# Layer 0's prompt attention with its values product turned round: values stationary, both branches' factors spread by a matmul

## The reference

```
o = g[..., 0:1] * o_cmp + g[..., 1:2] * o_slc + g[..., 2:3] * o_win
```

## Time and profile before

| | us |
|---|---|
| median of 3 runs | 3194.72 |
| lowest, highest | 3194.48, 3202.56 |
| the profiled execution | 3194.32 |
| its span, first to last instruction | 3192.5 |
| PE busy | 3044.4 (95%) |
| DVE busy | 1032.4 (32%) |
| ACT busy | 604.7 (19%) |
| POOL busy | 631.1 (20%) |
| prompt attention, first scores to first `z_total` matmul | 608.15 to 885.02 |

### The profile page before, as it was taken

One profiled execution on the slowest core, in us unless ns is written; L12 is line 12 of the kernel. 1 busy time (PEld: TensorE's weight loads), 2 busy tenths in 40 slices (PEclk: granted clock), 3 DMA queues, 4 the chain that ended last, 5 costly groups with the idle time before them and its releaser, 6 DMA issues.

```text
span 3192.5 us, 43230 instructions
## 1 busy us (share of the span) xinstructions
PE 3044.4 (95%) x18443; PEld 2762.8 (87%) x18443; DVE 1032.4 (32%) x2161; ACT 604.7 (19%) x1016; POOL 631.1 (20%) x298
## 2 busy tenths in 40 slices
PE   7999999999987999999999998988999999999997
PEld 5866767788844999999999998977899999999997
DVE  2003135665533342222222224065342122222224
ACT  3002111454432220000000003044220000000003
POOL 1020000000010232232232222202322223223220
PEclk9999999999998999999999999988999999999998
DMA  5634410210041311111111111100011111111111
GB/s 161 191 84 123 139 50 1 78 47 1 1 142 56 107 40 40 53 41 40 42 52 40 40 53 34 43 17 14 18 50 40 40 53 40 40 53 40 40 50 60
DMA packets 209617, 180.15 MB, mean 56 GB/s; under 512 B 36746, under 2 KB 190399, under 8 KB 208834
## 3 DMA queue, kind: packets, MB, share of 16 engines
q1 hardware_dynamic: 202416, 149.32, 15.6%
q0 software_dynamic: 6848, 28.04, 3.0%
q10 hardware_dynamic: 162, 0.04, 0.0%
HBM read 162.97 MB, written 19.51 MB: 57 GB/s over the span
## 4 chain that ended last, share of the span: by engine, by line
PE 87%; DVE 6%; SPq 3%; issue 2%; ACT 2%; DMA 1%; DVEq 0%; ACTq 0%
PE ps L1962 52%; PE ps L586 7%; PE ps L711 4%; PE ps L1411 3%; PE ps L1978 3%; PE ps L582 3%; PE ps L1381 2%; PE ps L1394 2%; PE ps L2343 2%; SPq L979 1%; SPq L977 1%; DVE arena L2056 1%; PE ps L2327 1%; PE ps L2206 1%; DVE arena L2072 1%
## 5 line engine op out<-in xcount | busy, mean ns | idle before, releaser
L1962 PE MATMUL ps<-spot,w_hi 128*128 128x368 f32 (+1 forms) x6828 | 1324.0, 328 | 18.5 <-DVE spot L2174 15.8
L1962 PEld LDWEIGHTS ps<-spot,w_hi 128*128 128x128 f32 x6828 | 1156.4, 188 | 23.0 <-DVE spot L2174 19.4
L1962 PE MATMUL ps<-spot,w_lo 128*128 128x368 f32 (+1 forms) x3468 | 763.7, 328 | 0.0
L1962 PEld LDWEIGHTS ps<-spot,w_lo 128*128 128x128 f32 x3468 | 599.1, 188 | 0.0
L1939 POOL CAST w_hi<-arena 128x2048 fp32r<-128x2048 f32 x79 | 153.6, 1944 | 1424.4 <-DMA arena<-in_w_gate_up 776.5
L1940 POOL TENSOR_TENSOR w_lo<-arena,w_hi 128x2048 fp32r<-128x2048 f32 x79 | 367.9, 4657 | 6.3
L2072 DVE TENSOR_TENSOR arena<-arena,ps 128x368 f32<-128x368 f32 x336 | 158.7, 528 | 486.2 <-PE ps L1962 460.1
L586 PE MATMUL ps<-arena 128*128 128x368 f32 (+1 forms) x768 | 244.2, 476 | 1.5 <-DVE arena L1210 1.5
L586 PEld LDWEIGHTS ps<-arena 128*128 128x128 f32 x768 | 146.5, 193 | 87.7 <-issue 5.5
L2149 ACT ACTIVATE arena<-arena 128x1088 f32<-128x1088 f32 x44 | 49.0, 1114 | 894.5 <-DVEq L2165 894.5
L2169 DVE TENSOR_TENSOR arena<-arena,ps 128x368 f32<-128x368 f32 x132 | 62.4, 528 | 446.9 <-PE ps L1962 441.8
(11 more groups left out here) (429 smaller groups left out, 2719.6 us busy)
## 6 DMA issues: line engine op xcount, KB each, us to landing
arena<-in_w_gate_up SPq DMA_DIRECT2D x88, 512.0 KB, 4.5
arena<-in_w_down SPq DMA_DIRECT2D x22, 1024.0 KB, 4.9
arena<-in_cache_nsa_cmp_kv SPq DMA_DIRECT2D x128, 128.0 KB, 2.2
arena<-in_cache_nsa_slc_kv SPq DMA_DIRECT2D x128, 128.0 KB, 2.5
arena<-in_w_in_even SPq DMA_DIRECT2D x9, 1024.0 KB, 6.3
x_spill<-arena POOLq DMA_DIRECT2D x1, 4352.0 KB, 14.9
arena<-in_x_prompt SPq DMA_DIRECT2D x8, 512.0 KB, 7.0
arena<-in_cmp_w_k POOLq DMA_DIRECT2D x16, 256.0 KB, 4.4
```

The lines of the kernel that those rows point to most:

```text
L1962: mm = nc.tensor.matmul(ps[:, 3 * s + j, 0:b - a], w, x[:, a:b], start=m == 0, stop=m == len(order) - 1)
```

## The change

The values product has its operands swapped: the 64 values of a key head are stationary (`v_of`) and the turned probabilities are moving. The result has head columns on partitions, g = 0 in PSUM's lower and g = 1 in its upper half, and tokens along the free axis. The values of a whole unit, both g by turns for each key tile, stand in one segment: behind the turn of chunk 0 and ahead of that of chunk 1.

The column of ones is gone. ACT's exponential sums up the denominators itself (`accum_out`, into `den4`). DVE's `factor_rows` makes reciprocal times gate of them, and PE's `factors` spreads these to the turned layout with four matmuls, whose stationary operand is a factor column repeated 64 times and whose moving one is the identity. ACT copies them to SBUF (`fac`). DVE's `finish` multiplies both branches by them in one product. The compressed matmul stands by itself (`compressed`) and ACT copies its result to `oN` (`base`). POOL adds the two branches and then adds them to `oN`, and gives `at_oT`. `mix`, `out`, POOL's copies and memsets and the semaphore `v_ones` go. PE's loop ends two steps earlier. SP waits in addition for the first `at_oT` ahead of its `dec_late` load, and DVE for the last `at_o` ahead of its first write to `rstd` in the decode attention, since `fac` lies in that tile.

```diff
--- before.py
+++ after.py
@@ -1296,15 +1296,17 @@
         ob = [at(h0 + 2 * T + 5376 + k * 256, 2, P) for k in range(2)]
         knew = at(16768, 2, TS)
         negm, scal = small[:, 0:8], small[:, 16:24]
+        fac = [rstd[:].rearrange("p a b -> p (a b)")[:, 256 * k:256 * (k + 1)] for k in range(2)]
+        den4 = [small[:, 24 + 4 * k:28 + 4 * k] for k in range(4)]
         loads["bias_in"] = [(bias_s, const["bias_slc"]), (bias_w, const["bias_win"])]
         UNITS = [(r, i, br) for r in range(R0) for i in range(PT) for br in range(2)]
 
         VA = HD + 2
 
-        def v_ones(br, i, g):
-
-            c = 256 * br + g * VA
-            return kvt[:, i, c:c + HD + 1]
+        def v_of(br, i, g):
+
+            c = 256 * br + P + g * HD
+            return kvt[:, i, c:c + HD]
 
         def key_tiles(u):
 
@@ -1331,17 +1333,16 @@
 
         def attn_pool(pool, E):
             pool.wait_ge(stored, 16 * stores[0])
-            pool.wait_ge(sem("kt_tr"), 2)
-            for br in range(2):
-                c = 256 * br
-                for g in range(G):
-                    E.chain(nc.gpsimd.tensor_copy(kvt[:, 0:PT, c + g * VA:c + g * VA + HD],
-                                                  kvt[:, 0:PT, c + P + g * HD:c + P + (g + 1) * HD]))
-                for g in range(G):
-                    nc.gpsimd.memset(kvt[:, 0:PT, c + g * VA + HD:c + g * VA + HD + 1], 1.0).then_inc(sem("v_ones"), 1)
             pool.wait_ge(sem("kt_s"), 1)
             for b in range(2):
                 window_load(pool, b)
+            for ri in range(len(UNITS) // 2):
+                r, i, _ = UNITS[2 * ri]
+                o = oN[:, r, toks(i)]
+                pool.wait_ge(sem("at_o"), ri + 1)
+                E.chain(nc.gpsimd.tensor_tensor(ob[ri % 2][:, 0], ob[ri % 2][:, 0], ob[ri % 2][:, 1], ALU.add))
+                pool.wait_ge(sem("at_base"), ri + 1)
+                nc.gpsimd.tensor_tensor(o, o, ob[ri % 2][:, 0], ALU.add).then_inc(sem("at_oT"), 1)
 
         def window_load(e, b):
             src = d["state_nsa_win_kv"][0, b].rearrange("(j p) a g e -> p j a (g e)", p=P)
@@ -1395,43 +1396,56 @@
                                                  sp3[u % 3][:, g, b * P:(b + 1) * P], ident[:])
                     mm.then_inc(sem(f"at_tr{g}"), 1)
 
-            def values(u, g):
+            def compressed(ri):
+                r, i, _ = UNITS[2 * ri]
+                if ri == 0:
+                    step_wait(pe, "dve", "pc")
+                if ri >= 2:
+                    pe.wait_ge(sem("at_o"), ri - 1)
+                nc.tensor.matmul(ps[:, 6 + ri % 2, 256:384], vbd[:, r], pcT[:, i], start=True, stop=True)\
+                    .then_inc(sem("at_cmp"), 1)
+
+            def values(u):
                 r, i, br = UNITS[u]
                 ri = u // 2
-                pe.wait_ge(sem(f"at_copied{g}"), first_chunk[u + 1])
-                if br == 0 and g == 0:
-                    if ri == 0:
-                        pe.wait_ge(sem("v_ones"), 4)
-                        step_wait(pe, "dve", "pc")
-                    if ri >= 2:
-                        pe.wait_ge(sem("at_oT"), ri - 1)
+                for g in range(G):
+                    pe.wait_ge(sem(f"at_copied{g}"), first_chunk[u + 1])
+                if br == 0:
+                    pe.wait_ge(sem("at_base"), ri + 1)
                 j0, n = key_tiles(u)
-                c = (2 * br + g) * VA
                 for j in range(n):
-                    mm = nc.tensor.matmul(ps[:, 6 + ri % 2, c:c + HD + 1], pt2[u % 2][:, g, j], v_ones(br, j0 + j, g),
-                                          start=j == 0, stop=j == n - 1)
+                    for g in range(G):
+                        mm = nc.tensor.matmul(ps[g * HD:(g + 1) * HD, 6 + ri % 2, br * P:(br + 1) * P], v_of(br, j0 + j, g),
+                                              pt2[u % 2][:, g, j], start=j == 0, stop=j == n - 1)
                 mm.then_inc(sem("at_pv"), 1)
 
-            def mix(ri):
-                r, i, _ = UNITS[2 * ri]
-                pe.wait_ge(sem("at_o"), ri + 1)
-                out = ps[:, 6 + ri % 2, 384:512]
-                nc.tensor.matmul(out, vbd[:, r], pcT[:, i], start=True, stop=False)
+            def factors(ri):
+
+                pe.wait_ge(sem("at_s"), ri + 1)
                 for br in range(2):
-                    mm = nc.tensor.matmul(out, ob[ri % 2][:, br], ident[:], start=False, stop=br == 1)
+                    for g in range(G):
+                        k = 4 * (ri % 2) + 2 * br + g
+                        mm = nc.tensor.matmul(ps[g * HD:(g + 1) * HD, 6 + ri % 2, (2 + br) * P:(3 + br) * P],
+                                              scal[:, k:k + 1].to_broadcast([P, HD]), ident[:], start=True, stop=True)
                 mm.then_inc(sem("at_ot"), 1)
 
-            for step in range(n_units + 5):
+            for step in range(n_units + 3):
                 if step < n_units:
                     score(step)
-                if step >= 6 and step % 2 == 0:
-                    mix(step // 2 - 3)
                 n_turn = len(chunks(step - 2)) if 2 <= step < n_units + 2 else 0
-                for c in range(2):
-                    if c < n_turn:
-                        turn(step - 2, c)
-                    if 3 <= step < n_units + 3:
-                        values(step - 3, c)
+                base = step // 2 - 1 if step % 2 == 0 and 2 <= step < n_units + 2 else None
+                if n_turn:
+                    turn(step - 2, 0)
+                if base is not None and n_turn < 2:
+                    compressed(base)
+                if step >= 3:
+                    values(step - 3)
+                    if step % 2 == 0:
+                        factors(step // 2 - 2)
+                if n_turn == 2:
+                    turn(step - 2, 1)
+                    if base is not None:
+                        compressed(base)
             pe.wait_ge(sem("z_summed"), R0 - 1)
             for k, (a, b) in enumerate(SPLIT):
                 mm = nc.tensor.matmul(ps[:, 2 + k, 0:b - a], ones[:], z_sum[:, a:b], start=True, stop=True)
@@ -1443,7 +1457,7 @@
             j, n = chunks(u)[c]
             e.wait_ge(sem(f"at_tr{g}"), k + 1)
             if u >= 2 and c == 0:
-                e.wait_ge(sem("at_pv"), 2 * (u - 2) + g + 1)
+                e.wait_ge(sem("at_pv"), u - 1)
             copy(pt2[u % 2][:, g, j:n], ps[:, 4 + g, 0:(n - j) * P].rearrange("p (j t) -> p j t", j=n - j))\
                 .then_inc(sem(f"at_copied{g}"), 1)
 
@@ -1472,20 +1486,26 @@
                 v.tensor_tensor_reduce(sp3[u % 3][:, g, 0:n], scores(u, g), bias[:, g, bias.shape[2] - n:], -1.0, -NEG,
                                        ALU.add, ALU.min, negm[:, m:m + 1]).then_inc(sem("at_scored"), 1)
 
-            def finish(ri):
+            def factor_rows(ri):
 
                 r, i, _ = UNITS[2 * ri]
-                dve.wait_ge(sem("at_pv"), 4 * ri + 4)
-                got = ps[:, 6 + ri % 2, 0:4 * VA].rearrange("p (k e) -> p k e", k=4)
+                dve.wait_ge(sem("at_exp"), 4 * ri + 4)
                 s = scal[:, 4 * (ri % 2):4 * (ri % 2) + 4]
-                ch(v.reciprocal(s, got[:, :, HD]))
+                if ri >= 2:
+                    dve.wait_ge(sem("at_ot"), ri - 1)
+                ch(v.reciprocal(s, den4[ri % 4]))
                 s4 = s.rearrange("p (b g) -> p b g", b=2)
                 gt = gates[:, i].rearrange("p (g r k) -> p k g r", g=G, r=R0)[:, 1:3, :, r]
-                ch(v.tensor_tensor(s4, s4, gt, ALU.mult))
+                v.tensor_tensor(s4, s4, gt, ALU.mult).then_inc(sem("at_s"), 1)
+
+            def finish(ri):
+
+                dve.wait_ge(sem("at_pv"), 2 * ri + 2)
+                dve.wait_ge(sem("at_fac"), ri + 1)
                 if ri >= 2:
-                    dve.wait_ge(sem("at_ot"), ri - 1)
-                v.tensor_tensor(ob[ri % 2].rearrange("p b (g e) -> p (b g) e", g=G), got[:, :, 0:HD],
-                                s.unsqueeze(2).to_broadcast([P, 4, HD]), ALU.mult).then_inc(sem("at_o"), 1)
+                    dve.wait_ge(sem("at_oT"), ri - 1)
+                v.tensor_tensor(ob[ri % 2].rearrange("p b t -> p (b t)"), ps[:, 6 + ri % 2, 0:2 * P], fac[ri % 2], ALU.mult)\
+                    .then_inc(sem("at_o"), 1)
 
             def new_rows():
                 dve.wait_ge(sem("kt_w"), 1)
@@ -1510,6 +1530,8 @@
                         score(step, c)
                     if 2 <= step < n_units + 2 and c < len(chunks(step - 2)):
                         copy_chunk(dve, v.tensor_copy, step - 2, c, 0)
+                if step >= 3 and step % 2 == 1 and step < n_units + 2:
+                    factor_rows(step // 2 - 1)
                 if step >= 5 and step % 2 == 1:
                     finish(step // 2 - 2)
                 if step in Z_STEPS:
@@ -1533,22 +1555,33 @@
                 n = key_tiles(u)[1] * P
                 act.wait_ge(sem("at_scored"), 2 * u + g + 1)
                 m = 2 * (u % 4) + g
```

(28 more changed lines are left out.)

## The result

| | before | after |
|---|---|---|
| median, us | 3197.22 (4 runs) | 3159.77 (4 runs, 3153.26 to 3165.99) |
| profiled execution, us | 3194.32 | 3159.47 |
| its span | 3192.5 | 3157.6 |
| first scores to first `z_total` matmul | 608.2 to 885.0: 276.8 | 613.0 to 853.0: 240.0 |

The ratio is 0.9889, 95% interval 0.9869 to 0.9910: 1.1% faster. The forecast was 3158 us. The median of before grew by one run measured beside the new ones; the forecast's 36.6 us was made against the profiled execution, and the profiled executions differ by 34.9.

What follows compares the result with a forecast made beforehand. PE's instruction stream was taken to bound the prompt attention. Values -56.5, passages +15.4, mix against factors -3.5 and new waits +8 made -36.6 us from the profiled 3194.32: forecast 3158 us, range 3144 to 3180.

Steps and rivals of the forecast that it cites:

- The values: Prompt attention's values with operands swapped: 1056 records at 0.0545 us in place of 0.108, saving 56.5 us.
- Rival (b): Halves don't overlap in the values: a record costs its 0.109 us stream, 3221 us, or load and stream, 3292; chance 0.05.
- the prediction's test of a round: PE's pieces in an attention round before, scores, transposes, values and mix, summed to 67.4 us; the third round took 68.5.
- The passages: PE's changes of matmul form around the values segment: 96 more at 0.16 us, +15.4 us; bounds 5 and 32.
- rival (c): Each passage costs PE the weight loader's 0.33 us: +16 us, 3174 us; chance 0.10.
- Factors against mix: PE drops 128 records that turned `ob`, 14.4 us, and adds 256 factor records at 0.0545 us, 14.0 us.
- Waits: PE's 3.1 us wait for `finish` goes; new waits for DVE in the attention add 8 us, bounds 2 and 18.
- rival (a): DVE takes PE's place as bound: score loops 0.5 us dearer in 32 large steps, +16 us, 3174 us; chance 0.10.
- part 7: New PE waits for DVE in large score steps, round-start bias scalings and gate products: 8 us together.
- ACT and POOL: Attention's sum readings at 0.186 us and copies on ACT, 64 sums of 0.3 to 0.7 us on POOL: all hidden.
- Behind the attention: Decode stage after `z_total`, led by SP's 80 page loads, moves as a whole, length unchanged; gain passed on in full.
- Rival (d): Decode stage gives the gain back if its loads, not `z_total`, set its end: about 3190 us; chance 0.05.

Runs made afterwards that it cites:

- block order: Changed kernel with all key tiles of g = 0 first, then all of g = 1, in the values: attention 269.1 us, median 3182.25 us.
- single half: Block-order kernel with both g of the values sent to the lower half of the array's columns, upper half's values left out: attention 290.8 us.

## Why the prediction was right

**The values (-56.5).** A record has the pitch read from the decode attention, 0.055 us. This is a property of form and order together, as the block order (+29 us) and the single half (+51 us) show. The change alternates, like the line in the earlier trace rows from which the prediction took its number, so the number was right; how much of it hung on the order the prediction did not say. Rival (b), no overlap, is what the single half shows: 0.110 us a record. Its mechanism was sound and its condition absent. The rule of the Trainium skill cited there ("TensorE: Matmul & The Clock Gate", Part 3), by which loads overlap only across row groups, does not hold in this form: both halves use all rows, and even in a single half a record took 0.110 us and not load and stream in sequence, 0.164. The same section of the Trainium skill also has loads pulled ahead into a background weight buffer, which would fit that 0.110; no run here shows it.

The other side of the term, the 0.108 us before, was a little high. It was read from one piece of twelve records, and shorter pieces of before cost less a record, as in the chain of the fourth round:

```profile
836.60 1.74 PE ps L1411 x16
...
841.12 0.84 PE ps L1411 x8
...
845.33 1.06 PE ps L1411 x10
```

Eight records take 0.105 us each, ten 0.106. Summed over all 96 pieces of the stretch before, the 1056 records take 112.8 us and not 114.0. So the values saved 112.8 - 1056 x 0.0545 = 55.2 us. (In the prediction's test of a round, 66 x 0.21 + 16 x 0.21 is 17.2 and not 17.4; nothing hangs on it.)

**The passages (+15.4).** Measured 0.147 us, so 96 come to 14.1. The matmul side was the right one to read; the loader's 0.33 of the earlier trace rows is not what PE pays, and rival (c) is out. So is a bound of 0.05. The Trainium skill ("TensorEngine Tiling (Array Packing)", Key Properties) has a change of tiling mode drain the engine; the trace agrees in that each change costs time, at two thirds of the 0.22 us that the prediction estimated for a full drain.

**Factors against mix (-0.4).** Eight records 0.44, as forecast.

**Waits (-3.1 + 8 = +4.9).** PE's waits went from 4.2 to 7.3 us, +3.1; some ten waits more at 0.15 would add 1.5. The size was allowed for rather than derived, but most of the waits stand where part 7 looked for them. Eight of 0.23 to 0.27 us, two a round, are before the first scores of i = 4 and of i = 5, 0.5 us a round where 0.8 was thought; three of 0.88 us are before a turn at the start of rounds 2 to 4, behind DVE's scaling of the bias tables. The scores of eight tiles have none. DVE is the engine that is late next, as rival (a) has it, at 6 of 7 us in all and not 16.

**The sum.** -55.2 + 14.1 - 0.4 + 3.1 + 1.5 = -36.9 for the stretch; 36.8 were measured. The 1.5 for starts behind waits is an estimate that no run isolates, so the sum is good to about 1 us. The forecast's -36.6 came as close because its errors cancel: the values 1.3 us too large a gain, the passages 1.3 us too dear, the waits 0.3 us too many. The total of the medians fell by 37.5 us, with the runs spread over some 13 us, so its match with the forecast to 2 us is in part luck.

**ACT and POOL (0).** Readings 0.195 us each instead of 0.186; with no sums nothing moves. POOL's sums take 0.54 and 0.50 us, inside 0.3 to 0.7. The last one starts at 854.60 and ends at 855.05, and PE turns the decode's first keys at 856.61: hidden with 1.6 us over.

**Behind the attention (0).** SP's 80 page loads start 7.5 us behind the first `z_total` matmul, as before (7.4), and take 92.72 us. Rival (d) is out: the stage moved as a whole. Over thirteen profiles, of before, the changed kernel and its variants, what follows the attention takes 2296 to 2312 us with no relation to the edit. That spread, more than the attention, is what limits the totals.

## What to carry to other kernels

Where PE's stream is the bound and a matmul moves fewer columns than it loads weights (here 65 against 128), try its operands swapped: this took 55 us off the values and, with all that it brought along, 36.8 us off the stretch. Let neighbouring matmuls alternate between the halves of the array's columns, in runs of at most four records; keep them in one segment, since each passage to another shape costs 0.15 us, and put it where it covers a copy that the next PE work waits for. Then look at which engine is late next before shortening PE further: here a further 7 us off PE gave 3.8.

## What the runs showed of the hardware

PE overlaps the two column halves beyond neighbours: runs of four records for each half cost 1.5 us (241.5 against 240.0 us), runs of eight 18 us, and one half alone twice the time of two a record. A change of half hides about 3.5 records. I had expected the order to cost all of 56 us or nothing.

The same 64 records of the decode's last values (L1725 before, L1759 after) took 6.28 us in the profile of before and 3.71 us in that of after, most of the 3.3 us by which that stage got shorter. The granted clock of the windows around them was 0.58 and 1.00: the 1.2 GHz level for most of the first, the 2.4 GHz level in the second. PE had waited alike ahead of them, 4.14 and 1.80 us in two stops before, 4.14 and 1.70 us after, so the two profiles show the same work at either level. The two windows (columns as in the earlier trace rows), before,

```profile
1024.00:1030.80 6.80, 6.36 (x66) 6.22 (x68) 0.00 (x0) 0.30 (x2) 0.00 (x0) 0.58 0.00 0
```

and after:

```profile
991.50:995.40 3.90, 3.79 (x66) 3.64 (x68) 0.00 (x0) 0.00 (x0) 0.00 (x0) 1.00 0.02 4
```

Gains of this kind come and go with the execution: in the second profile of the changed kernel the decode stage up to these records took 145.0 us, in the first 142.1 and in that of before 145.4.
